# Two side-by-side products for 13 blocks of a split-float decoder kernel

## The chip, the cores and the metric

The kernel is one program on one core of a Trainium2 chip. The metric is the device time of that program in microseconds (us). The engines are TensorE (PE, with its weight loads shown as PEld), VectorE (DVE), ScalarE (ACT), GpSimd (POOL) and SyncE (SP), which issues most DMAs.

## The reference, cut to what matters

Two decoder blocks run over 256 tokens with a model width of 2048, in float32. Everything heavy is a product of activations with a weight matrix:

```python
proj = xn @ w_in                                   # hgrn_qf, hgrn_v, gate_q_k, idx_q, attn_v ...
h = h + jnp.concatenate([y_h, y_a], axis=-1) @ w_out       # mix_out
h = h + memory_cross_attention(...)                # cross_q, cross_k, cross_v, cross_out
h = h + sqrelu_mlp(rms_norm(h, norm_mlp), w_up, w_down)    # up0..3, down0..3
# second block: pooling mixer (pool_*, out0), shared keys and values of a sparse attention
kv = (hn @ w_kv)                                   # cmp_kv, sel_k, sel_v, win_k, win_v
q = hn @ w_b[:, :1536]                             # nsa_q, 3 blocks
```

RMS norms stand before the products. The kernel multiplies by the norm's factor of each token behind the product, when it reads the result.

## The kernel before

**Blocks and units.** The weights pass through the core once, in 95 blocks, one after the other in the order of `plan_stream`. A dense block is 2048 rows by 512 columns of a weight matrix (4 MB). It comes in 4 DMAs of 1 MB into 4 slots of `ring` (SP, `stream`, L474), each 4 row tiles of 128 rows by 512 columns, so a run of 2 KB per row. A block is worked on in 8 units of 2 row tiles. For each unit ACT rounds the weights into `w_high` (`high_unit`, L1244), POOL subtracts to get the rest, `w_low` (`low_parts`, L628, line L654, in 2 pieces of 512 elements per partition or 4 of 256), and PE multiplies. `w_high` and `w_low` have 4 places (`UNITS`), so ACT starts unit n when PE is done with unit n - 4 (`units_used`), and DMA of a ring slot starts when POOL is done with it (`low_ready`).

**The products.** A float32 product is made of three products of rounded parts: w_high x_high + w_high x_low + w_low x_high (`accumulate`, L687 is its matmul). In a features unit (L691) the weights are the stationary operand and the 256 tokens stream: 2 row tiles x 4 feature tiles x 3 products = 24 matmuls of 256 columns, 192 per block. In a tokens unit the tokens are stationary and 512 features stream: 12 matmuls of 512 columns, 96 per block.

**Groups.** The sums of a dense block stand in 2 banks of PSUM, 256 tokens x 4 feature tiles. That is a group, and groups take turns on two pairs of banks (`pair_of`). Before PE begins group g it waits until group g - 2 has been read out (`group_free`, L671, semaphore `evacuated`). DVE reads a group out with two operations of 512 elements (`read_out` L1691, called by `keep` L1699, lines L1736 and L1731; or `residual_group` L1750, which adds to `hT`).

**Order around the change.** Each engine runs its own written list. In `hgrn_qf` (4 blocks, the first work of the kernel) DVE can read out the first group only when the norm's factor is known: `norm_sum` (L792, lines L795 and L797) stands in PE's list before unit 4 of block 1, ACT makes the root (L1288, L1289), and DVE waits for it (`scale_known`). In the second half DVE's list reads `keep("cmp_kv")`, `rope_angles`, `build_blocks(0)` (L2352), `low_blocks(0)` (L2362, which waits for ACT's L1596), `keep("sel_k")`, `build_blocks(1)`, `low_blocks(1)`, `keep("sel_v")`, two `rotate` (L2322 to L2326), `keep("win_k")`. In `nsa_q` (3 blocks) DVE rotates queries (`rotate`) after each block; the first attention steps on PE (L818) wait for the last two.

Of the kernel before, what the change touches and what calls it, by code (L numbers as in the profile page):

```python
# [12 lines left out]
P = 128  # L13
# [35 lines left out]
class Gemm:  # L49
# [6 lines left out]
    def __init__(self, b0, blocks, g0, groups, rows, width):  # L56
        self.b0, self.blocks, self.g0, self.groups, self.rows, self.width = b0, blocks, g0, groups, rows, width
        self.units = 8 * blocks // groups

# [4 lines left out]
    def unit(self, u):  # L64

        half = (self.rows + 1) // 2
        return (0, half) if u % 2 == 0 else (half, self.rows - half)


def plan_stream():  # L70
# [12 lines left out]
    for name, blocks, groups, *shape in order:  # L83
        plan[name] = Gemm(b, blocks, g, groups, *(shape or (4, 512)))
        b += blocks
        g += groups
# [3 lines left out]
def build_program(nc, a):  # L90
    PLAN = plan_stream()
    ctx = ExitStack()
    with ctx:
# [14 lines left out]
        x_high = sb("x_high", [P, KT, T], F32R)  # L108
        x_low = sb("x_low", [P, KT, T], F32R)
# [347 lines left out]
        def _(sp):  # L457
# [16 lines left out]
            def stream(name, source):  # L474
# [3 lines left out]
                def block_of(n, b, more):  # L478
                    for j in range(4):

                        need = 8 * b + 2 * j - 2 * RING + 2
                        if need > 0:
                            sp.wait_ge(low_ready, need + more)
                        dst = ring[:, j, 0:g.rows * g.width].rearrange("p (k n) -> p k n", k=g.rows)
# [8 lines left out]
                peel = g.blocks if g.blocks < 3 or name == "out0" else int(g.b0 == 0)  # L493
# [6 lines left out]
            def columns(w, col0):  # L500
# [3 lines left out]
                return lambda n, j: w3[:, 4 * j:4 * j + 4, bass.ds(n * 512 + col0, 512)]  # L504
# [49 lines left out]
            stream("out0", lambda n, j: out0_part(n, GATED_FIRST[j]))  # L554
# [115 lines left out]
        def _(pe):  # L670
# [33 lines left out]

            def tokens_unit(g, b, u, pair, x, first, of, more=0):
# [27 lines left out]
            def product(name, unit, x, made=None, ready=x_ready, sums=None, begun=0, sums_at=7):  # L733
# [3 lines left out]
                def block_of(n, more, more_groups, wait):  # L737
                    group_free(g.g0 + n, more_groups)
                    for u in range(8):
# [4 lines left out]
                        unit(g, g.b0 + n, u, pair_of(g.g0 + n), x, 4 * (u // 2), KT, more)  # L744

                peel = g.blocks if g.blocks < 4 else (begun if made is None else 2)
# [115 lines left out]
            def one_unit(name, k):  # L862

                g, n, u = PLAN[name], k // 8, k % 8
                if u == 0:
# [35 lines left out]
            for n in range(4):  # L901
                group_free(g.g0 + n)
                for u in range(8):
                    if n == 0:
                        pe.wait_ge(rows_kept, u + 1)
                    if n == 1 and u == 4:
                        norm_sum(pair_tile(16, 16), columns=True)
                    features_unit(g, g.b0 + n, u, pair_of(g.g0 + n), operand, 4 * (u // 2), KT)
# [298 lines left out]
            def turn_h(i):  # L1207

                pe.wait_ge(evacuated, PLAN["out0"].g0 + 4)
# [21 lines left out]
        def _(act):  # L1231
# [72 lines left out]
            def norm_turn(name, slot, cols, squares=scratch, freed=0, begun=0):  # L1304
# [3 lines left out]
                for u in range(8):  # L1308
# [3 lines left out]
                    elif u == 0:  # L1312
                        act.wait_ge(evacuated, g.g0 + 3)
# [5 lines left out]
                act.wait_ge(evacuated, g.g0 + 4)  # L1319
# [143 lines left out]
            for c in range(2):  # L1463
                act.wait_ge(evacuated, c + 1)
                act.activation(hg_gates[:, c, :], pair_tile(4 * c, 4), ACT.Sigmoid).then_inc(hg_act, 1)
                high(1)
            for c in range(2):
                act.wait_ge(evacuated, c + 3)
# [213 lines left out]
        def _(dve):  # L1682
# [8 lines left out]
            def read_out(g, q, i, put):  # L1691

                n = g.g0 + q
# [5 lines left out]
            def keep(name, dst):  # L1699
# [812 lines left out]
```

## Time and profile before

| | us |
|---|---|
| median of 3 runs | 2368.94 (2368.47 to 2369.37) |
| the profiled execution | 2373.35 |
| its span (first to last instruction) | 2371.6 |
| PE busy | 2300.8 |
| POOL busy | 2076.7 |
| ACT busy | 1072.3 |
| DVE busy | 934.6 |

1.75 us of the profiled execution lie outside its span. Engines run at the same time, so busy times don't add up. Matmuls are pipelined: each shows the time from its start to the end of its last column, and the next starts well before that; what a matmul costs in a row of them is the distance from start to start. The granted clock is PE's: 1.00 is 2.4 GHz and 0.50 is 1.2 GHz.

### The profile page before, as it was taken

The page shows a single profiled execution, that of the slowest core. Times are in us where ns is not written, and L with a number is a line of the kernel's source. Part 1 is how long each engine was busy: PE and PEld are TensorE (multiplying, and loading weights), DVE is VectorE, ACT ScalarE, POOL GpSimd, SP SyncE. Part 2 cuts the span into 40 slices and gives each one's busy share as a digit, 9 for nine tenths or more (in the row PEclk, how much of TensorE's full clock was granted, in tenths as well). Part 3 has the DMA queues.
Part 4 walks back from the last instruction along what each step waited for, and adds up shares of the span by engine and source line. Part 5 has one row for each costly group of instructions (what it writes and reads, how often), then busy time and mean ns, then how long its engine had stood idle before and what let it go on. Part 6 is the DMA issues. An engine that isn't in the chain of part 4 may idle for free. (4 is left out here: it accounts for less than half of the span.)

```text
span 2371.6 us, 38269 instructions
## 1 busy us (share of the span) xinstructions
PE 2300.8 (97%) x14870; PEld 2082.1 (88%) x14870; DVE 934.6 (39%) x1389; ACT 1072.3 (45%) x1412; POOL 2076.7 (88%) x1933
## 2 busy tenths in 40 slices
PE   8999999999999999999999999999999998999998
PEld 8989998788997888888888888999899987999886
DVE  5165665765053620120120121522514555465522
ACT  5443334474365533333333333544445445455553
POOL 8999998797996899999999999898999898875587
PEclk9999999999999999999999999999999999999999
DMA  6654444353543456565655555554455556543343
GB/s 233 186 168 147 157 144 151 143 194 126 196 160 125 152 186 202 189 194 187 188 193 188 187 192 178 165 188 151 144 197 189 176 167 201 166 154 107 107 160 124
DMA packets 207143, 401.09 MB, mean 169 GB/s; under 512 B 10515, under 2 KB 21013, under 8 KB 206357
## 3 DMA queue, kind: packets, MB, share of 16 engines
q1 hardware_dynamic: 206628, 398.45, 52.2%
q8 instruction: 104, 1.70, 0.3%
q10 hardware_dynamic: 368, 0.59, 0.1%
q14 instruction: 43, 0.34, 0.1%
HBM read 396.92 MB, written 2.10 MB: 168 GB/s over the span
## 5 line engine op out<-in xcount | busy, mean ns | idle before, releaser
L654 POOL TENSOR_TENSOR w_low<-ring,w_high 128x512 fp32r<-128x512 f32 (+3 forms) x1868 | 2067.5, 1132 | 278.2 <-ACT w_high L1253 217.8
L1253 ACT ACTIVATE w_high<-ring 128x1024 fp32r<-128x1024 f32 (+2 forms) x760 | 788.9, 1040 | 1206.7 <-PE bank L687 1192.8
L687 PE MATMUL bank<-x_high,w_high 128*128 128x256 f32 x2948 | 850.8, 289 | 23.3 <-POOL w_low L654 11.6
L687 PE MATMUL bank<-x_low,w_high 128*128 128x256 f32 x2948 | 836.5, 284 | 0.0
L687 PE MATMUL bank<-x_high,w_low 128*128 128x256 f32 x2948 | 836.5, 284 | 0.0
L687 PEld LDWEIGHTS bank<-x_high,w_high 128*128 128x128 f32 x2948 | 565.7, 192 | 32.7 <-issue 21.4
L687 PEld LDWEIGHTS bank<-x_low,w_high 128*128 128x128 f32 x2948 | 566.0, 192 | 0.9 <-issue 0.5
L687 PEld LDWEIGHTS bank<-x_high,w_low 128*128 128x128 f32 x2948 | 565.7, 192 | 0.1
L687 PE MATMUL bank<-w_high,x_high 128*128 128x512 f32 x928 | 373.2, 402 | 7.4 <-POOL w_low L654 4.3
L687 PE MATMUL bank<-w_low,x_high 128*128 128x512 f32 x928 | 363.3, 391 | 0.0
L687 PE MATMUL bank<-w_high,x_low 128*128 128x512 f32 x928 | 363.0, 391 | 0.0
L687 PE MATMUL bank<-w_high,hidden 128*128 128x512 f32 x960 | 296.2, 390 | 0.0
L687 PEld LDWEIGHTS bank<-w_high,x_high 128*128 128x128 f32 x928 | 175.1, 189 | 54.3 <-issue 7.4
L687 PEld LDWEIGHTS bank<-w_high,hidden 128*128 128x128 f32 x960 | 179.7, 188 | 37.1
L687 PEld LDWEIGHTS bank<-w_low,x_high 128*128 128x128 f32 x928 | 174.9, 188 | 37.5
L687 PEld LDWEIGHTS bank<-w_high,x_low 128*128 128x128 f32 x928 | 175.1, 189 | 37.0 <-issue 2.9
L687 PE MATMUL bank<-w_low,hidden 128*128 128x512 f32 x480 | 186.9, 389 | 0.0
L1736 DVE TENSOR_TENSOR proj<-bank,scale_all 128x512 f32<-128x512 f32 (+1 forms) x62 | 39.8, 683 | 179.7 <-PE bank L687 178.0
L1792 DVE SCALAR_TENSOR_TENSOR x_low<-hT,gains,x_high 128x256 fp32r<-128x256 f32 x80 | 93.2, 1217 | 36.7 <-ACT x_high L1300 36.5
L687 PEld LDWEIGHTS bank<-w_low,hidden 128*128 128x128 f32 x480 | 90.1, 188 | 18.8
L2209 DVE TENSOR_SCALAR heads_scratch<-bank,scale_all 128x512 f32<-128x512 f32 x32 | 22.6, 747 | 202.4 <-issue 194.3
L1744 DVE TENSOR_TENSOR proj<-bank,proj 128x512 f32 (+1 forms) x22 | 14.2, 686 | 181.1 <-PE bank L687 181.1
(299 smaller groups left out, 1740.2 us busy)
## 6 DMA issues: line engine op xcount, KB each, us to landing
ring<-in_w_in SPq DMA_DIRECT2D x64, 1024.0 KB, 5.4
ring<-in_w_up SPq DMA_DIRECT2D x64, 1024.0 KB, 5.2
ring<-in_w_down SPq DMA_DIRECT2D x64, 1024.0 KB, 5.1
ring<-in_w_out SPq DMA_DIRECT2D x48, 1024.0 KB, 5.1
ring<-in_a_w_in SPq DMA_DIRECT2D x32, 1024.0 KB, 5.3
ring<-in_b_w_in SPq DMA_DIRECT2D x32, 1024.0 KB, 5.4
ring<-in_w_kv SPq DMA_DIRECT2D x24, 1024.0 KB, 5.2
ring<-in_w_mem_kv SPq DMA_DIRECT2D x16, 1024.0 KB, 5.1
```

The source lines that it names most:

```text
L654: last = pool.tensor_tensor(w_low[:, u % UNITS, part], ring[:, u // 2, first:first + n], w_high[:, u % UNITS, part], ALU.subtract)
L687: mm = pe.matmul(out, lhs, rhs, start=start and n == 0, stop=stop and n == 2, skip_group_check=True)
L1253: act.activation(w_high[:, u % UNITS, 0:n], ring[:, u // 2, r0 * g.width:r0 * g.width + n], ACT.Copy)\
L1736: return lambda n, c, b: dve.tensor_tensor(proj[:, bass.ds(n * 4 + (t0 + 2 * c), 2), :], two(b), scale_two, ALU.mult)
L1744: return lambda n, c, b: dve.tensor_tensor(v[:, c, bass.ds(n * 512, 512)], b[:, :], v[:, c, bass.ds(n * 512, 512)], ALU.add)
L1792: last = dve.scalar_tensor_tensor(out=x_low[:, t, :], in0=hT[:, t, :], scalar=gains[:, slot, cols.start + t:cols.start + t + 1], in1=x_hig ...
L2209: last = dve.tensor_scalar(up_rows[:, h, :], bank[2 * ((g.g0 + q) % 2) + h][:, :], scale_col(h), 0.0, ALU.mult, ALU.max)
```

## The change

Thirteen of the features blocks become wide: blocks 1, 2, 3 of `hgrn_qf`; 1, 2 of `mix_out`; 1, 2 of `out0`; 1 of `cmp_kv`; `sel_k`; `win_k`; and 0, 1, 2 of `nsa_q`. `x_high` and `x_low` become two halves of one tensor `x_parts`. A wide unit has 4 row tiles of 256 features in place of 2 row tiles of 512. For each row tile and feature tile w_high streams x high and low in one matmul of 512 columns, into a whole bank (high in columns 0 to 255, low in 256 to 511), and w_low streams x_high into columns 0 to 255: 16 matmuls per unit.

```diff
+WIDE = {"hgrn_qf": (1, 2, 3), "mix_out": (1, 2), "out0": (1, 2), "cmp_kv": (1,), "sel_k": (0,), "win_k": (0,),
+        "nsa_q": (0, 1, 2)}
...
+            def wide_unit(g, n, u):
+
+                half, v = divmod(u, 4)
+                if v == 0:
+                    group_free(g.group(n) + half)
+                pe.wait_ge(low_ready, 8 * (g.b0 + n) + u + 1)
...
+                for k in range(4):
+                    kt = 4 * v + k
+                    for f in range(2):
+                        cols = slice(f * P, f * P + P)
+                        pe.matmul(pair[f][:, :].rearrange("p (a t) -> p a t", a=2), wh[:, k, cols], x_parts[:, :, kt, :],
+                                  start=(kt == 0), stop=(kt == KT - 1), skip_group_check=True)
+                        mm = pe.matmul(pair[f][:, 0:T], wl[:, k, cols], x_high[:, kt, :], start=False,
+                                       stop=(kt == KT - 1), skip_group_check=True)
+                mm.then_inc(units_used, 1)
```

A wide block has two groups of 256 features, one for units 0 to 3 and one for units 4 to 7, so `group_free` is asked in the middle of a block too, and the block's sums fill 4 banks in turn rather than 2. DVE reads a wide group out with 4 operations of 256 elements that scale, a wait for them, and 2 that add high and low (`read_wide`), or, into `hT`, with 2 adds, a wait and 2 adds:

```diff
+            def read_wide(g, n, t0, factor=None):
+
+                for half in range(2):
+                    pair = pair_rows(g.group(n) + half)
+                    t = t0 + 4 * n + 2 * half
+                    dve.wait_ge(units_used, 8 * (g.b0 + n) + 4 * half + 4)
+                    for b, f in ((pair[0], 0), (pair[1], 1)):
+                        for dst, src in ((proj[:, t + f, :], b[:, T:2 * T]), (b[:, 0:T], b[:, 0:T])):
+                            if factor is None:
+                                last = dve.tensor_tensor(dst, src, scale_rows_, ALU.mult)
...
+                    then(last)
+                    for f in range(2):
+                        last = dve.tensor_tensor(proj[:, t + f, :], pair[f][:, 0:T], proj[:, t + f, :], ALU.add)
+                    last.then_inc(evacuated, 1)
```

The ring DMAs of wide blocks bring 8 row tiles x 256 columns, so runs of 1 KB, 1 MB each as before. Blocks of `mix_out`, `out0`, and the others named are written out instead of looped on PE, SP and DVE. The waits that counted groups (`evacuated`) are renumbered.

Two places of the new order. On PE, the middle of block 1 of `hgrn_qf` (units 3 and 4), before:

```order
L687 MATMUL bank3<-x_high,w_high 128x256
L687 MATMUL bank3<-x_low,w_high 128x256
L687 MATMUL bank3<-x_high,w_low 128x256
L795 MATMUL bank4<-proj,ones 128x256 [waits norm_folded]
L797 MATMUL bank4<-ones,proj 128x2 x2
L687 MATMUL bank2<-x_high,w_high 128x256 [waits low_ready]
L687 MATMUL bank2<-x_low,w_high 128x256
L687 MATMUL bank2<-x_high,w_low 128x256
```

The same place after the change:

```order
L741 MATMUL bank3<-x_parts,w_high 128x512
L743 MATMUL bank3<-x_parts,w_low 128x256
L841 MATMUL bank4<-proj,ones 128x256 [waits norm_folded]
L843 MATMUL bank4<-ones,proj 128x2 x2
L741 MATMUL bank0<-x_parts,w_high 128x512 [waits low_ready,evacuated]
L743 MATMUL bank0<-x_parts,w_low 128x256
```

Unit 4 went on in banks 2 and 3 and waited for its weights alone; now it begins a group in banks 0 and 1 and waits for `evacuated` as well, which is the read-out of block 0.

On DVE, from the end of `build_blocks(0)` to the start of `build_blocks(1)`, before:

```order
L2352 TENSOR_TENSOR heads_scratch<-proj,pe_cols 128x16x15 x7
L2362 TENSOR_TENSOR block_parts_50<-heads_scratch,block_parts_50 128x1920 [waits blocks_high]
L1731 SCALAR_TENSOR_TENSOR proj<-bank0,scale_all 128x512 [waits units_used]
L1731 SCALAR_TENSOR_TENSOR proj<-bank1,scale_all 128x512
L2352 TENSOR_TENSOR heads_scratch<-proj,pe_cols 128x16x15 [waits x_ready,evacuated]
```

and after:

```order
L2438 TENSOR_TENSOR heads_scratch<-proj,pe_cols 128x16x15 x7
L2448 TENSOR_TENSOR block_parts_50<-heads_scratch,block_parts_50 128x1920 [waits blocks_high]
L1763 SCALAR_TENSOR_TENSOR proj<-bank0,scale_all 128x256 [waits units_used]
L1763 SCALAR_TENSOR_TENSOR bank0<-bank0,scale_all 128x256
L1763 SCALAR_TENSOR_TENSOR proj<-bank1,scale_all 128x256
L1763 SCALAR_TENSOR_TENSOR bank1<-bank1,scale_all 128x256
L1767 TENSOR_TENSOR proj<-bank0,proj 128x256 [waits dve_order]
L1767 TENSOR_TENSOR proj<-bank1,proj 128x256
L1763 SCALAR_TENSOR_TENSOR proj<-bank2,scale_all 128x256 [waits units_used]
```

The read-out of `sel_k` keeps its place in DVE's list and grows from 2 operations to 12, in two groups. `sel_k` was one group, so the block behind it, `sel_v`, waited for the last group of `cmp_kv`; now `sel_k` is two groups, and `sel_v` waits for the first of them.

## Rows read from the trace of the kernel before

**Rows 1.** Page, part 1: engine, busy us (share of span), instructions
```profile
PE 2300.8 (97%) x14870; PEld 2082.1 (88%) x14870; DVE 934.6 (39%) x1389; ACT 1072.3 (45%) x1412; POOL 2076.7 (88%) x1933
```

**Rows 2.** Windows: stretch, length, busy us (count) by engine, PE clock, DMA share, GB/s
```profile
65.43:88.47 23.04, 23.04 (x195) 23.04 (x193) 1.29 (x2) 8.49 (x8) 21.43 (x18) 1.00 0.62 188
952.43:974.20 21.77, 21.77 (x98) 18.02 (x97) 1.29 (x2) 8.49 (x8) 20.28 (x17) 1.00 0.62 193
1846.73:1870.78 24.05, 23.96 (x198) 23.39 (x196) 1.76 (x3) 10.16 (x11) 22.90 (x18) 1.00 0.55 176
1893.91:1919.80 25.89, 22.92 (x98) 17.52 (x97) 18.47 (x15) 15.77 (x15) 22.12 (x15) 1.00 0.51 163
1919.80:1944.15 24.35, 23.81 (x192) 23.30 (x193) 10.12 (x11) 7.43 (x7) 23.72 (x17) 1.00 0.51 161
```

**Rows 3.** Timeline of POOL, mix_out to cross_q: start, us, operation [idle before, releaser]
```profile
631.25 2.55 POOL L654 TENSOR_TENSOR w_low<-ring,w_high 128x512 fp32r<-128x512 f32 x2 [0.16 <-POOL w_low L654]
...
661.56 6.09 POOL L654 TENSOR_TENSOR w_low<-ring,w_high 128x512 fp32r<-128x512 f32 x6 [0.16 <-POOL w_low L654]
```

**Rows 4.** Timeline of POOL, then of PE, in cross_q
```profile
662.81 30.33 POOL L654 TENSOR_TENSOR w_low<-ring,w_high 128x512 fp32r<-128x512 f32 x34
...
689.57 0.36 PE L687 MATMUL bank<-x_high,w_high 128*128 128x256 f32 x1 [0.22 <-POOL w_low L654]
```

**Rows 5.** Timelines of PE, ACT and DVE around unit 4 of hgrn_qf's block 1
```profile
52.58 0.28 PE L687 MATMUL bank<-x_high,w_low 128*128 128x256 f32 x1
52.94 0.70 PE L795 MATMUL bank<-proj,ones 128*128 128x256 f32 x2
53.47 0.50 PE L797 MATMUL bank<-ones,proj 128*128 128x2 f32 x4
53.84 0.36 PE L687 MATMUL bank<-x_high,w_high 128*128 128x256 f32 x1
...
55.27 0.48 ACT L1288 ACTIVATE scale_all<-bank,eps_col 128x260 f32<-128x260 f32 x1
55.76 1.28 ACT L1289 ACT_TABLE_LOAD   x1
57.06 0.42 ACT L1289 ACTIVATE scale_all<-scale_all 128x260 f32<-128x260 f32 x1
...
57.83 1.29 DVE L1736 TENSOR_TENSOR proj<-bank,scale_all 128x512 f32 x2 [1.54 <-ACT scale_all L1289]
```

**Rows 6.** Timelines of DVE, ACT and PE from the end of cmp_kv into sel_v
```profile
1870.31 1.29 DVE L1736 TENSOR_TENSOR proj<-bank,scale_all 128x512 f32<-128x512 f32 x2 [22.02 <-PE bank L687]
...
1894.23 1.81 ACT L1596 ACTIVATE block_parts<-heads_scratch 128x1920 fp32r<-128x1920 f32 x1 [4.82 <-DVE heads_scratch L2352]
...
1896.08 2.16 DVE L2362 TENSOR_TENSOR block_parts<-heads_scratch,block_parts 128x1920 fp32r<-128x1920 f32 x1 [1.88 <-ACT block_parts L1596]
1898.15 1.28 DVE L1731 SCALAR_TENSOR_TENSOR proj<-bank,scale_all 128x512 f32<-128x512 f32 x2
...
1901.05 0.50 PE L687 MATMUL bank<-w_high,x_high 128*128 128x512 f32 x1 [1.50 <-POOL w_low L654]
```

**Rows 7.** Groups by line and form, DVE reading PSUM: count, busy us, mean ns, idle before
```profile
L1863 DVE SCALAR_TENSOR_TENSOR x_low<-bank,gains,x_high 128x256 fp32r<-128x256 f32 x64 | 27.7, 477 | 41.2 <-ACT x_high L1399 40.9 <-DVE x_low L1863 0.2
L1935 DVE COPY proj<-bank 128x256 f32<-128x256 f32 x32 | 13.4, 419 | 43.4 <-PE bank L858 43.3
```

**Rows 8.** Windows and timeline of PE around an idle stretch before nsa_q, columns as in 2 and 3
```profile
2003.20:2006.40 3.20, 0.00 (x0) 0.00 (x0) 0.42 (x1) 1.51 (x2) 2.48 (x2) 1.00 1.05 395
2007.40:2010.80 3.40, 3.40 (x19) 3.40 (x18) 0.00 (x0) 1.31 (x2) 3.24 (x4) 0.50 0.93 305
2010.80:2013.70 2.90, 2.90 (x26) 2.90 (x25) 0.00 (x0) 1.06 (x1) 2.74 (x3) 0.99 0.93 321
...
2006.47 0.35 PE L687 MATMUL bank<-x_high,w_high 128*128 128x256 f32 x1 [3.27 <-POOL w_low L654]
```

**Rows 9.** Timelines of DVE and PE from the last group of nsa_q to attention
```profile
2084.20 1.29 DVE L1736 TENSOR_TENSOR proj<-bank,scale_all 128x512 f32<-128x512 f32 x2 [11.56 <-PE bank L687]
...
2092.58 1.11 DVE L2326 TENSOR_TENSOR proj<-rstd 32x512 f32<-32x512 f32 x1
...
2093.75 0.92 PE L818 MATMUL bank<-proj 128*128 128x128 f32 x4 [0.51 <-DVE proj L2326]
```

**Rows 10.** DMA issues: count, KB each, median us to landing; and an ACT wait for one
```profile
ring<-in_w_kv SPq DMA_DIRECT2D x24, 1024.0 KB, 5.2
ring<-in_cmp_w SPq DMA_DIRECT2D x8, 1024.0 KB, 5.6
...
2002.70 2.00 ACT L1253 ACTIVATE w_high<-ring 128x1024 fp32r<-128x1024 f32 x2 [2.02 <-DMA ring<-in_b_w_in]
```

**Rows 11.** Timeline of DVE behind hgrn_qf: the last group, and the wait for PE
```profile
111.84 1.29 DVE L1736 TENSOR_TENSOR proj<-bank,scale_all 128x512 f32 x2 [21.75 <-PE bank L687]
...
147.68 0.77 DVE L2017 COPY_PREDICATED heads_scratch<-ident,bank 128x512 f32<-128x512 int32 x1 [9.21 <-PE bank L919]
```

More of the change, by code:

```diff
@@ L58, in __init__, with group, ended @@
         self.units = 8 * blocks // groups
+        self.wide = ()
+    def group(self, n):
+        return self.g0 + n + sum(1 for w in self.wide if w < n)
+    def ended(self, n):
+        return self.group(n + 1)
     def made(self, n=0):
@@ L553, in _ @@
             out0_part = columns(w_out2[0:D, :], 0)
-            stream("out0", lambda n, j: out0_part(n, GATED_FIRST[j]))
+            stream("out0", lambda n, j, wide=False: out0_part(n, j if wide else GATED_FIRST[j], wide))
             w_kv = a["w_kv_2"]
@@ L737, in block_of @@
                 def block_of(n, more, more_groups, wait):
-                    group_free(g.g0 + n, more_groups)
+                    if n in g.wide:
+                        for u in range(8):
+                            wide_unit(g, n, u)
+                        return
+                    group_free(g.group(n), more_groups)
                     for u in range(8):
@@ L743, in block_of @@
                             pe.wait_ge(ready, made + u // 2 + 1)
-                        unit(g, g.b0 + n, u, pair_of(g.g0 + n), x, 4 * (u // 2), KT, more)
-                peel = g.blocks if g.blocks < 4 else (begun if made is None else 2)
+                        unit(g, g.b0 + n, u, pair_of(g.group(n)), x, 4 * (u // 2), KT, more)
+                peel = g.blocks if g.blocks < 4 or g.wide else (begun if made is None else 2)
                 for n in range(begun, peel):
@@ L1752, in residual_group @@
                 g = PLAN[name]
+                if j in g.wide:
+                    for half in range(2):
+                        pair = pair_rows(g.group(j) + half)
+                        dve.wait_ge(units_used, 8 * (g.b0 + j) + 4 * half + 4)
+                        for part in range(2):
+                            for f in range(2):
+                                h = hT[:, 4 * j + 2 * half + f, :]
+                                last = dve.tensor_tensor(h, pair[f][:, part * T:part * T + T], h, ALU.add)
+                            if part == 0:
+                                then(last)
+                        last.then_inc(evacuated, 1)
+                    return
                 dve.wait_ge(units_used, g.made(j))
```

72 lines of the change are left out of this document (48 added, 24 removed).

## Prediction

> **What bounds the kernel now.** I read the page's busy times first: PE is busy 97% of the span and POOL 88% [rows 1]. So PE's list sets the time, with POOL close behind. Then the windows of single blocks, for the price of a matmul. In a features block 192 matmuls of 256 columns take 23.04 us, 0.120 us each; in a tokens block 96 of 512 columns take 21.77 us, 0.2268 us each [rows 2]. Twice the columns cost 0.1068 us more, so a matmul costs 0.1068 us per 256 columns and 0.0132 us for being one. The chain of waits has little in it but PE; what counts is where PE would wait, so I went along the 13 blocks and asked of each new wait in PE's list when it ends, by the timelines of the engine waited for.
>
> **Term 1, the matmuls.** A row tile and feature tile cost 3 x 0.120 = 0.360 us before, and 0.2268 + 0.120 = 0.3468 after, 0.0132 less. A dense block has 64 such pairs: 0.85 us, 22.19 in place of 23.04. Thirteen blocks give 11.0 us if nothing else moves. No row shows a stream made of two pieces of 256 columns; its bounds are 0.2268 (like one piece) and 0.240 (like two matmuls). I take the first, since one instruction and one load are issued.
> The Trainium skill has a rule against this term ("TensorE: Matmul & The Clock Gate", "Back-to-back issue gap"): a matmul in a warm stream costs its columns and about 2.5 ns. By it the pair would save 2.5 ns, 64 x 13 of them 2.1 us. These rows have 13.2 ns, for 256 and for 512 columns alike, so the trace disagrees with it here.
>
> **Term 2, a wait inside hgrn_qf.** Unit 4 of block 1 now opens a group in the banks of block 0, so PE waits for DVE to read block 0 out. DVE can't before the norm's factor is there, and `norm_sum` stands right before that wait in PE's own list. In the rows: PE issues it at 52.94, ACT's root ends at 57.48, DVE reads out from 57.83 to 59.12, and PE went on at 53.84 [rows 5]. The old kernel needed this read-out only at 65.4, at block 2. In the new one PE reaches unit 4 0.4 us sooner (four units at 2.77), which ACT can use for its table load, so the read-out ends near 58.7, and PE resumes at 58.75: 4.9 us of idle PE. Behind the wait stand all later matmuls; ACT and POOL are at most four units ahead, so they stop too. Idle PE has a second price. After 3.27 us of idle PE the granted clock was 0.50 for 3.4 us, 19 matmuls ran in that stretch against 26 in the 2.9 us behind it [rows 8]; at 0.50 a stretch of 3.4 us does the work of about 1.9, so 1.5 us. Sum for the stage: 4.9 + 1.5 - 3 x 0.85 = **+3.9 us**. The read-out of the last group is 1.2 us longer (term 5), but the next PE work that needs DVE starts at 147.7 after DVE had waited 9.2 us for PE [rows 11], so that stays covered.
>
> **Term 3, mix_out and out0.** Four blocks, 3.4 us at most. POOL is the cover to check. Its unit in these loops takes 2.55 and 0.16 of wait, 2.71 [rows 3]; PE's new unit takes 2.77, so POOL still keeps ahead, by 0.06 instead of 0.17 a unit. In `out0` POOL has since saturated its four places before `cmp_kv` needs them, so its 1.7 us stay. Behind `mix_out` stands `cross_q`, where POOL works without a gap from 662.81 for 30.33 us and PE waits 0.22 us for it [rows 4]. POOL had slack (the 0.16 waits are its own, the pieces from 652.9 on waited for PE) of about 0.8 us to start that stretch sooner. So PE gets 1.7 sooner to that wait and loses 0.9 there. I take **-0.8** for `mix_out` and **-1.7** for `out0`.
>
> **Term 4, sel_v waits for sel_k.** `cmp_kv` block 1 saves 0.85. But `sel_v` must now wait for the first half of `sel_k` to be read out, and in DVE's list this stands behind `rope_angles`, `build_blocks(0)` and `low_blocks(0)`. Before, that read-out began at 1898.15 [rows 6], while `sel_v` began at 1893.91 [rows 2] and needed only `cmp_kv`. New times, with S for the shift of PE at the end of `cmp_kv`: its own last group takes 1.2 us longer (term 5), so the chain read-out, angles, blocks, ACT L1596, L2362 ends at 1899.4 + S; six operations of 0.40 us and a wait, 2.5 us; PE starts `sel_v` at 1902.0 + S. It would be ready at 1870.78 + 22.19 = 1893.0 + S: 9 us idle, and 1.5 for the clock. From there: `sel_v` 21.77, `win_k` 22.19, together 1947.6 + S, if POOL keeps up. POOL has some 36 us of subtractions from `sel_v` unit 4 on and can't start them before 1907.2, so it is just in time; I add 0.5. Before, `win_k` ended at 1944.15 [rows 2]. That is +4.0 + S, S = -0.85: **+3.15 us**. It is less than the 9 us of the stall because the old kernel lost 4.1 us in `sel_v` (25.89 against 21.77) and 1.3 in `win_k` (24.35 against 23.04) to POOL and ACT [rows 2, 6], and these waits go: POOL works ahead during the stall. The savings of `sel_k` and `win_k` are in the sum. The work behind is paced by PE's units and by ACT, and keeps the shift.
>
> **Term 5, DVE.** A group of 512 elements x 2 takes 1.29 us [rows 6]. A 256-element operation reading PSUM takes 0.42 (copy) to 0.48 us (three operands) alone [rows 7], in a row some 0.40 to 0.43: six of them 2.4 and a semaphore round 0.1, so 2.5 per wide group, 1.2 more behind the last unit. Per wide block DVE does 5.0 us instead of 1.3. DVE has 39% of work [rows 1] and these operations lie beside matmuls, except behind a last group. That counts in `nsa_q`: the last group, two rotations, and the attention step that waits 0.51 us for them [rows 9]. So of the 3 x 0.85 saved there 1.2 go back. The cover elsewhere, if gone, costs PE a wait at `group_free` of at most that 2.5 us per place.
>
> **Term 6, DMA.** Runs of 1 KB in place of 2: `cmp_w`, which has such runs, lands in 5.6 us, `w_kv` in 5.2 [rows 10]. Where slots are refilled a block ahead that is nothing. At the start of `nsa_q` ACT waited 2.02 us for a landing and PE for ACT [rows 8, 10], so I charge 0.5 us. With term 5, `nsa_q`: -2.55 + 1.2 + 0.5 = **-0.8**. Renumbered waits, unrolled loops and the common tensor of x cost nothing that a row shows: sequencers wait there anyway; at most a few tenths.
>
> **Sum.** 3.9 - 0.8 - 1.7 + 3.15 - 0.8 = +3.75. On the profiled execution: span 2371.6 + 3.75, and 1.75 outside it, 2377.1. The median of the runs is 4.41 below that execution (2368.94 against 2373.35), so **2372.7 us**.
>
> **The rivals.**
> A, as forecast: both stalls come and eat the gain. Its own range is 2369 to 2377: no clock loss at either stall takes 3.0 off, POOL not held up in `cross_q` 0.9; and on the other side the clock staying low twice as long adds 3.0 and a late POOL behind `sel_v` 1.
> B, the stalls are largely absorbed. The place is `sel_v`: everything from there to `nsa_q` is paced by POOL and by ACT's place in its list, so PE ahead of them is worth nothing, and PE late costs nothing until POOL's four places are full. If `win_k` then ends where it ended (term 4 gives -0.85 or 0 instead of +3.15) and the wait in `hgrn_qf` costs no clock, the time is 2372.7 - 4.0 - 1.5 - 1.5 = 2366; with a shorter root chain 2363. For it: POOL leads by only 0.1 us in that stretch. Against: a 9 us hole is longer than the 5.4 us of waits that it can replace.
> C, slower: the two-piece stream costs like two matmuls, 0.240. Then term 1 is gone everywhere it counted, some 8 to 9 us, and the stalls stay: 2381. Each 0.001 us more on a stream costs 64 x 10 blocks of it, 0.64 us, so it decides from 0.2284 on, where the time passes 2373.7. For it: nothing shows such a stream. Against: it is one instruction.
> By the Trainium skill's rule of term 1 ("TensorE: Matmul & The Clock Gate", "Back-to-back issue gap"), the saving is 2.1 us in place of 11.0 and the time nearly the same as in C, 2381; the rows against it are [rows 2], and I give it 2 of C's 10 in a hundred.
> D, slower: the read-outs of wide groups cost more than 2.5 us, since half of them write back into PSUM, which no row shows; at 4 us each the three chains behind last groups (`cmp_kv`, `sel_k`, `nsa_q`) lose 1.5 to 3 us each: 2378.
> E, the change does what it says and the wait in `hgrn_qf` is shorter, for example as ACT's root is earlier: no place in the rows for it, since ACT did it as soon as its table was loaded.
>
> **How the numbers follow.** A 0.55, B 0.17 (with E), C 0.10, D 0.18. A measurement of this kernel can tell about 0.2% from no change, 4.7 us: below 2364.2 is faster, above 2373.7 slower. A lies two thirds below 2373.7 and one third above; B is a third faster and else the same; C and D are slower. With some weight for unseen gains: faster 0.12, same 0.47, slower 0.41. The range leaves out the far end of B, and C: 2364 to 2380.5.
>
> **What would show it right or wrong.** The timeline of PE must show some 5 us idle before unit 4 of `hgrn_qf` block 1 near 54 us, released by DVE, and some 9 us before `sel_v`, each followed by a few us at clock 0.50. Wide blocks without waits must take 22.2 us; 23.0 would be C. DVE's groups of wide blocks must take near 2.5 us; 4 would be D. If `win_k` ends no later relative to `cmp_kv` than before, B holds. Where a wide block in `nsa_q`, `mix_out` or `out0` begins a group late, a cover that I counted on is gone.

## The result and the profile after

The changed kernel takes 2375.22 us (median of 12 runs, 2372.48 to 2378.5), the one before 2371.29 us in the same comparison (12 runs, 2368.47 to 2374.59). The ratio is 1.0016, 95% interval 1.0009 to 1.0024: slower by 0.16%, 3.9 us, where the prediction had +3.75 us. The forecast time was 2372.7 us, inside its range of 2364 to 2380.5 and 2.5 below the median; 2.35 of that is the kernel before itself, 2368.94 in three runs ahead of the prediction and 2371.29 here. The profiled execution after has a span of 2373.4 us, 1.8 us more than the one before. The two differences need not agree: executions of one kernel differ by several us here, and below I say which part of that the traces show.

The busy times first, as in [rows 1]:

```profile
PE 2293.9 (97%) x14038; PEld 2038.2 (86%) x14038; DVE 962.7 (41%) x1503; ACT 1073.0 (45%) x1412; POOL 2076.7 (87%) x1933
```

832 matmuls have gone and PE is busy 6.9 us less, in a kernel that takes longer. So PE waits more. The waits of PE over the whole program (line that waited, who released it: us in total, times, longest):

```profile
PE bank L711 <- POOL w_low L678: 11.0, 16, 1.4
PE bank L711 <- DVE proj L1767: 7.9, 1, 7.9
...
PE bank L741 <- DVE proj L1810: 4.7, 1, 4.7
...
PE bank L741 <- POOL w_low L678: 2.9, 1, 2.9
```

Two single waits for DVE are new, 4.7 and 7.9 us. The waits for POOL, 17.2 us in 21 places before, are 13.9 now. Then the windows by block (columns as in [rows 2]): block 1 and 2 of `hgrn_qf`, `mix_out` 1, `cmp_kv` 1, `sel_k`, `sel_v`, `win_k`:

```profile
40.20:71.58 31.38, 26.43 (x136) 22.64 (x135) 15.63 (x15) 15.34 (x16) 23.50 (x17) 0.89 0.46 136
71.58:93.77 22.19, 22.19 (x130) 19.40 (x129) 4.36 (x12) 8.50 (x8) 20.70 (x18) 1.00 0.62 190
604.45:627.06 22.61, 22.61 (x130) 19.62 (x129) 2.79 (x6) 8.50 (x8) 21.34 (x18) 1.00 0.62 200
...
1848.62:1871.94 23.32, 23.19 (x134) 19.65 (x132) 3.94 (x10) 10.19 (x11) 22.17 (x18) 1.00 0.56 180
1871.94:1902.32 30.38, 22.46 (x131) 19.55 (x128) 28.13 (x31) 13.35 (x17) 26.03 (x19) 0.91 0.54 173
1902.32:1926.32 24.00, 24.00 (x96) 19.64 (x97) 8.94 (x15) 9.13 (x8) 19.22 (x16) 0.91 0.43 133
1926.32:1948.92 22.60, 22.60 (x129) 19.61 (x128) 13.94 (x19) 8.49 (x8) 22.05 (x16) 1.00 0.55 180
```

Read the length, PE's busy time and the clock together. `hgrn_qf` 2 is the clear case, 22.19 us with PE busy all the time. `mix_out` 1 is as clear and takes 22.61. In block 1 of `hgrn_qf` and in `sel_k` PE is busy 5 and 8 us less than the block is long, and the clock falls below 1.00. By stages, from the first matmul of one block to the first of another:

| stage | before | after | difference | predicted |
|---|---|---|---|---|
| hgrn_qf 1 to 3 | 70.33 | 75.76 | +5.43 | +3.9 |
| mix_out 1, 2 with 3 and cross_q | 96.19 | 96.09 | -0.1 | -0.8 |
| out0 1, 2 with 3 and cmp_kv 0 | 93.19 | 93.05 | -0.1 | -1.7 |
| cmp_kv 1 to win_k | 97.42 | 100.30 | +2.88 | +3.15 |
| nsa_q with nsa_zq 0 | 110.62 | 108.23 | -2.39 | -0.8 |

These are +5.7 us together. The rest of the way to +1.8 lies in blocks that the change does not touch: `attn_v` 0 took 40.57 us before and 38.42 after, as a stretch at clock 0.50 near 386 us is missing after; the first block began 1.25 us sooner behind its first DMA; `cmp_hid_k` and the gates are 0.6 us shorter. The stretch before, with PE's clock at 0.76 on the mean of it:

```profile
383.00:390.00 7.00, 5.08 (x13) 3.69 (x14) 2.08 (x1) 4.79 (x6) 6.84 (x11) 0.76 0.58 179
```

That one need not be chance. In all 13 traces of the changed kernel and its versions below, `attn_v` 0 takes 38.3 to 38.9 us and the clock does not fall there; PE's wait for ACT, 2.07 us before, is 1.3 to 1.7 in twelve of them and 2.0 in that of run 4. The start of block 1 of `hgrn_qf`, 41.2 before and 40.2 after, lies anywhere from 39.8 to 42.2 us in these traces.

**The wait in hgrn_qf**, to be held against [rows 5]. Timelines of PE, ACT and DVE:

```profile
51.97 0.70 PE L841 MATMUL bank<-proj,ones 128*128 128x256 f32 x2 [0.29 <-DVE proj L1895]
52.50 0.50 PE L843 MATMUL bank<-ones,proj 128*128 128x2 f32 x4
57.67 0.79 PE L741 MATMUL bank<-x_parts,w_high 128*128 128x512 f32 x1 [4.67 <-DVE proj L1810]
...
55.87 0.42 ACT L1342 ACTIVATE scale_all<-scale_all 128x260 f32<-128x260 f32 x1
...
56.33 1.29 DVE L1810 TENSOR_TENSOR proj<-bank,scale_all 128x512 f32<-128x512 f32 x2 [1.00 <-ACT scale_all L1342]
```

And the window behind the wait:

```profile
57.70:63.60 5.90, 5.90 (x19) 5.03 (x20) 2.00 (x6) 0.35 (x1) 0.64 (x1) 0.50 0.61 178
```

The norm's sum, the root, the read-out, and then unit 4, 5.7 us after the norm matmul began; before, unit 4 followed it by 0.9 us. That window has 5.9 us at clock 0.50, so 3 us are lost there on top of the 4.67 of idle time.

**The wait before sel_v**, against [rows 6]. DVE and PE:

```profile
1871.47 0.42 DVE L1761 TENSOR_TENSOR proj<-bank,scale_all 128x256 f32<-128x256 f32 x1 [8.88 <-PE bank L743]
...
1885.21 10.91 DVE L2438 TENSOR_TENSOR heads_scratch<-proj,pe_cols 128x240 f32<-128x240 f32 x8
1897.99 2.16 DVE L2448 TENSOR_TENSOR block_parts<-heads_scratch,block_parts 128x1920 fp32r<-128x1920 f32 x1 [1.87 <-ACT block_parts L1649]
1900.06 0.42 DVE L1763 SCALAR_TENSOR_TENSOR proj<-bank,scale_all 128x256 f32<-128x256 f32 x1
...
1901.52 0.75 DVE L1767 TENSOR_TENSOR proj<-bank,proj 128x256 f32<-128x256 f32 x2
...
1902.32 1.22 PE L711 MATMUL bank<-w_high,x_parts 128*128 128x512 f32 x2 [7.92 <-DVE proj L1767]
```

DVE has no idle time between `cmp_kv` and this read-out but for 1.87 us, and PE starts `sel_v` when its first half is out. A wide group takes 1900.06 to 1902.27, 2.2 us.

### The profile page after: what moved, and what is told of

The parts are those of the page before. It is cut to its first block and busy times, and to the rows that moved or that the text cites. A ratio compares the mean times of both kernels' runs of the same rounds, so it can differ in the third digit from the quotient of the medians.

```text
span 2373.4 us, 36567 instructions
## 1 busy us (share of the span) xinstructions
PE 2293.9 (97%) x14038; PEld 2038.2 (86%) x14038; DVE 962.7 (41%) x1503; ACT 1073.0 (45%) x1412; POOL 2076.7 (87%) x1933
## 5 line engine op out<-in xcount | busy, mean ns | idle before, releaser
L711 PE MATMUL bank<-x_parts,w_high 128*128 128x256 f32 x4232 | 782.2, 287 | 16.7 <-POOL w_low L678 7.0
L711 PEld LDWEIGHTS bank<-x_parts,w_high 128*128 128x128 f32 x4232 | 660.0, 192 | 25.6 <-issue 14.1
L711 PE MATMUL bank<-x_parts,w_low 128*128 128x256 f32 (+1 forms) x2116 | 600.0, 284 | 0.0
L711 PE MATMUL bank<-w_high,x_parts 128*128 128x512 f32 x1856 | 585.4, 397 | 13.8 <-DVE proj L1767 7.9
L711 PEld LDWEIGHTS bank<-w_high,x_parts 128*128 128x128 f32 x1856 | 346.0, 189 | 96.9 <-issue 10.0
L711 PEld LDWEIGHTS bank<-x_parts,w_low 128*128 128x128 f32 (+1 forms) x2116 | 405.0, 191 | 0.1
L711 PE MATMUL bank<-w_low,x_parts 128*128 128x512 f32 x928 | 363.2, 391 | 0.0
L741 PE MATMUL bank<-x_parts,w_high 128*128 128x512 f32 x832 | 296.8, 401 | 7.7 <-DVE proj L1810 4.7
L743 PE MATMUL bank<-x_parts,w_low 128*128 128x256 f32 x832 | 233.9, 281 | 0.0
L711 PEld LDWEIGHTS bank<-w_low,x_parts 128*128 128x128 f32 x928 | 175.0, 189 | 37.6
L741 PEld LDWEIGHTS bank<-x_parts,w_high 128*128 128x128 f32 x832 | 157.5, 189 | 46.0 <-DVE proj L1810 4.8
```

The source lines that it names most:

```text
L711: mm = pe.matmul(out, lhs, rhs, start=start and n == 0, stop=stop and n == 2, skip_group_check=True)
L741: pe.matmul(pair[f][:, :].rearrange("p (a t) -> p a t", a=2), wh[:, k, cols], x_parts[:, :, kt, :], start=(kt == 0), stop=(kt == KT - 1), ...
L743: mm = pe.matmul(pair[f][:, 0:T], wl[:, k, cols], x_high[:, kt, :], start=False, stop=(kt == KT - 1), skip_group_check=True)
```

## The experiments

In runs 1 to 8 the time is that of one execution, the profiled one, and single executions of one kernel lie up to 6 us apart. So stages are compared, not whole times: a whole time carries stretches at half clock that come and go.

**1. Block 1 of hgrn_qf narrow.**

```diff
-WIDE = {"hgrn_qf": (1, 2, 3),
+WIDE = {"hgrn_qf": (2, 3),
...
-                if n == 0:
-                    group_free(g.g0)
+                if n not in g.wide:
+                    group_free(g.group(n))
...
```

> Block 1 of hgrn_qf is narrow again; 12 blocks stay wide. My theory (PE idles for the read-out of block 0 and then runs at half clock): that block takes 24.3 us as before the change, not 31.4, so the stage is 7.1 us shorter, no 4.7 us hole near 53 us, clock 1.00 there; blocks 2 and 3 keep 22.2 to 22.6 us. The half-clock stretch in attn_v near 386 us that the changed kernel lacks may return, 2 us, so 5 to 7 us less in all than the changed kernel. Rival (the hole is only work moved, and ACT and POOL catch up behind it): hgrn_v starts at most 1 us sooner.

Time 2369.73 us. The window of blocks 1 to 3:

```profile
40.49:109.97 69.48, 69.41 (x457) 63.14 (x455) 21.36 (x29) 36.33 (x36) 64.62 (x50) 1.00 0.60 183
```

69.48 us against 75.76, without idle time and at clock 1.00. Making this one block wide costs 6.3 us net. Two wide blocks without it are 0.85 us better than before the change. The wait for the read-out is shown as the cause: without it `hgrn_v` starts 6 us sooner, where the rival allowed 1. I had expected 7.1; blocks 2 and 3 took 22.61 and 22.62 us in this kernel instead of 22.19 (section 8 is on that). The stretch at half clock in `attn_v` that might have returned did not.

**2. sel_k narrow.** In `WIDE`:

```diff
-        "sel_k": (0,),
```

> sel_k is narrow again, one group; 12 blocks stay wide. From the start of cmp_kv block 1 to the start of win_v the kernel before took 97.4 us and the changed one 100.3. My theory (sel_v waits for a read-out that stands late in VectorE's list): no hole before sel_v, the POOL and ACT waits of 4 to 5 us in sel_v and win_k are back, and the stretch takes 97.5 us, 2.8 less. Rival (VectorE's longer read-outs as such cost the time, by delaying its chain): sel_k's own read-out is a third of them, so the stretch stays above 99 us.

Time 2367.89 us. From `cmp_kv` 1 to the start of `win_v`:

```profile
1842.74:1939.94 97.20, 93.60 (x550) 81.41 (x549) 59.43 (x62) 40.93 (x43) 90.48 (x65) 0.98 0.53 170
```

97.20 us, 3.1 less than after the change and 0.2 less than before it. The rival, over 99 us, falls. With `cmp_kv` 1 and `win_k` still wide, 0.9 to 1.7 us should have been gained; `sel_v` took 26.57 and `win_k` 24.18, so POOL and ACT keep it, as rival B had said of that stretch.

**3. What part of the price is the clock.** Matmuls whose results nobody reads keep PE busy during the two waits, 8 in the first and 14 in the second.

```diff
+            def fill(to, count):
+                for i in range(count):
+                    pe.matmul(bank[to][:, 0:T], ones[:, :], hT[:, i, :], start=True, stop=True, skip_group_check=True)
...
+                if g is PLAN["hgrn_qf"] and n == 1 and u == 4:
+                    fill(6, 8)
...
+            fill(7, 14)
             product("sel_v", tokens_unit, operand)
```

> The changed kernel with PE kept at work in its two holes: 8 matmuls of ones with a tile of hT into an unused bank before the wait in hgrn_qf block 1, and 14 before sel_v. Nothing reads them. My theory (a hole costs its own length and then a stretch at half clock): the holes end at the same times, the clock stays at 1.00, hgrn_qf block 1 takes 31.4 - 3 = 28.4 us and sel_v 24.0 - 2 = 22 us, 5 us less in all. Rival (the clock falls for another reason, or the half-clock stretch is hidden by waits behind it): block 1 within 0.5 us of 31.4.

Time 2371.4 us. Block 1 of `hgrn_qf`, and `sel_v`:

```profile
40.70:69.37 28.67, 27.28 (x153) 23.29 (x151) 15.61 (x15) 15.34 (x16) 23.49 (x17) 1.00 0.50 150
...
1898.13:1921.67 23.54, 23.54 (x97) 19.27 (x97) 9.94 (x15) 9.14 (x8) 19.44 (x16) 0.93 0.44 137
```

In `hgrn_qf` the clock stayed at 1.00 and the block took 28.67 us instead of 31.38: 2.7 us of the price were the clock, 4.7 the wait itself. Before `sel_v` it worked in part only: the fillers ended before the wait did, PE was idle for 1.9 us, 3.4 us at 0.50 followed, and `sel_v` took 23.54 instead of the 22.0 that I expected. That half is inconclusive.

**4. Wide groups, but three matmuls.** w_high streams x high and low in two matmuls of 256, all else as changed.

```diff
-                        pe.matmul(pair[f][:, :]..., wh[:, k, cols], x_parts[:, :, kt, :],
-                                  start=(kt == 0), stop=(kt == KT - 1), ...)
+                        pe.matmul(pair[f][:, 0:T], wh[:, k, cols], x_high[:, kt, :],
+                                  start=(kt == 0), stop=False, ...)
+                        pe.matmul(pair[f][:, T:2 * T], wh[:, k, cols], x_low[:, kt, :],
+                                  start=False, stop=(kt == KT - 1), ...)
```

> The changed kernel with its layout, groups, DMAs, waits and read-outs, but w_high streams x_high and x_low in two matmuls of 256 columns: 24 matmuls per unit as before the change. My theory (the pair of streams saves 7 to 13 ns, the price of one instruction, the rest of the change only costs): clear wide blocks take 23.04 us instead of 22.19 or 22.61; the kernel is 4 to 8 us slower than the changed one, about 2381, the holes stay. Rival (the 256-column and two-half layout saves the time): the blocks stay near 22.2 to 22.6.

Time 2377.51 us. Clear wide blocks took 23.04 us, as narrow ones, so the groups of 256 features and the 1 KB runs of the DMAs cost PE nothing there, and the whole gain is the saved matmul. The time is 2.3 us above the changed kernel's median, less than the 4 to 8 that I expected, since one of the two holes, which were to stay, nearly closed. Three other stages taught more. `cross_q` and `cmp_kv` 0 went back to 27.10 and 24.07 us, from 27.82 and 24.79: what they lost after the change came with an earlier PE (run 7 adds to this for `cmp_kv` 0). `nsa_zq` 0 stayed at 33.52 (33.09 before, 33.56 after), so the 0.4 to 0.5 us there are the longer read-out and its rotations. And the wait before `sel_v` shrank from 7.9 to 2.1 us, which no theory had; `sel_k` took 25.79 us instead of 30.38. The window of `sel_k` in this kernel, then timelines of DVE and POOL in it:

```profile
1874.56:1900.35 25.79, 23.55 (x196) 23.14 (x193) 21.54 (x31) 12.39 (x15) 25.16 (x16) 1.00 0.52 163
```
```profile
1887.09 3.95 DVE L2440 TENSOR_TENSOR heads_scratch<-proj,pe_cols 128x240 f32<-128x240 f32 x8
...
1886.85 5.31 POOL L678 TENSOR_TENSOR w_low<-ring,w_high 128x512 fp32r<-128x512 f32 x1
```

The same eight operations of `build_blocks(0)` that took 10.91 us after (and 10.93 before) take 3.95 here, while one subtraction of POOL takes 5.31 instead of some 1.3. After the change DVE and POOL took turns, one operation each, at 1.36 us per operation of DVE (10.91 for eight), and POOL's took 1.4 to 1.5; here DVE went through in one go and POOL stood. What decides between the two was not tried. By the Trainium skill ("Advanced Engine Details and Errata", "GPSIMD Details") the Pool engine shares a read and a write interface with VectorE and conflicts, among others, with its instructions of two SBUF inputs; the eight operations of DVE here read two tensors in SBUF, `proj` and `pe_cols`, and the rows agree, while read-outs, which take one input from PSUM, stay at 0.42 us beside POOL.

**5. The read-outs of sel_k earlier in DVE's list.** `read_wide` gets the halves that it reads.

```diff
             rope_angles()
+            read_wide(PLAN["sel_k"], 0, 8, -ATT_SCALE, (0,))
             build_blocks(0)
             low_blocks(0)
-            keep("sel_k", scaled_keys(8), 8, -ATT_SCALE)
+            read_wide(PLAN["sel_k"], 0, 8, -ATT_SCALE, (1,))
```

> Everything as changed, with only the read-outs of sel_k moved earlier in the list of DVE (first half ahead of build_blocks(0), second behind low_blocks(0)). Theory: the idle time ahead of sel_v falls from 7.9 us to 6 to 7 us, the stretch from cmp_kv 1 to win_v from 100.3 to 99 to 100 us. Rival (order does not matter): 100.3 again.

Time 2376.42 us, with clock stretches elsewhere that the stage does not contain. The windows of `sel_k` and `sel_v`, and PE's longest wait in them:

```profile
1874.25:1896.55 22.30, 22.30 (x131) 19.66 (x129) 21.92 (x27) 7.56 (x11) 21.67 (x17) 1.00 0.58 190
1896.55:1924.35 27.80, 23.89 (x99) 18.94 (x97) 20.36 (x21) 15.50 (x15) 22.99 (x16) 0.94 0.45 151
```
```profile
PE bank L711 <- POOL w_low L678: 3.1, 1, 3.1
```

`sel_k` runs through in 22.30 us, and the stage takes 97.39 us instead of 100.30; I had expected 99 to 100. PE no longer waits for DVE there, where I expected 6 to 7 us of it, but for POOL, 3.1 us and then 0.8. I had thought that the second half of `sel_k` would hold `sel_v` as the first had, but `sel_v` needs only the first. The place of the first read-out in DVE's list is the cause of that hole. But 97.39 us is what the stage took before the change (97.42) and with `sel_k` narrow (97.20): closing the hole brings the stage back to where it was, and POOL keeps what the wide blocks save.

**6. Blocks 1 and 2 of out0 with three matmuls.** The edit of 4, only where `g is PLAN["out0"]`.

> In blocks 1 and 2 of out0 alone w_high streams x high and low in two matmuls again (24 per unit, in wide groups); all else as changed. Theory (cmp_kv 0 waits for the norm chain of DVE, ACT and PE, whose end does not depend on how fast out0 runs): blocks 1 and 2 of out0 take 23.04 us each instead of 22.61, cmp_kv 0 takes 24.07 instead of 24.79, so the stretch from out0 1 to cmp_kv 1 is 93.2 us, as before the change (93.2) and 0.1 us above the changed kernel (93.06). Rival (the 0.72 us in cmp_kv 0 come from the longer read-outs of the wide blocks): cmp_kv 0 stays at 24.8 and the stretch grows to 93.9.

Time 2377.05 us. `out0` 1, and `cmp_kv` 0:

```profile
1754.76:1777.80 23.04, 23.04 (x195) 23.04 (x194) 2.80 (x6) 8.47 (x8) 21.77 (x18) 1.00 0.63 199
1823.88:1847.95 24.07, 24.07 (x200) 23.92 (x199) 20.20 (x16) 13.63 (x18) 20.72 (x13) 1.00 0.52 173
```

As the theory said, 93.19 us from `out0` 1 to `cmp_kv` 1, 0.14 more than after the change. What `out0` gained, `cmp_kv` 0 gave back. In the changed kernel the place is PE's wait before the norm of `cmp_kv`:

```profile
1844.77 0.70 PE L841 MATMUL bank<-scratch,ones 128*128 128x256 f32 x2 [0.61 <-DVE scratch L1895]
```

**7. The order of the four matmuls of a row tile.**

```diff
                     for f in range(2):
                         pe.matmul(pair[f]..., wh..., x_parts...)
-                        mm = pe.matmul(pair[f][:, 0:T], wl..., x_high...)
+                    for f in range(2):
+                        ...
+                        mm = pe.matmul(pair[f][:, 0:T], wl..., x_high...)
```

> Within a row tile the two matmuls of 512 columns go first and the two of 256 behind them, instead of 512, 256, 512, 256; all else as changed. Theory (each matmul costs its columns plus about 13 ns whatever stands next to it): four matmuls take 692 to 708 ns as now, clear wide blocks 22.2 to 22.6 us. Rival (a short matmul behind a long one hides part of its weight load, and two short ones in a row do not): four matmuls take over 710 ns, blocks over 22.7.

Time 2371.24 us. `mix_out` 1, and `cross_q`:

```profile
603.03:625.33 22.30, 22.30 (x131) 19.46 (x129) 2.80 (x6) 8.51 (x8) 21.03 (x18) 1.00 0.62 202
670.66:699.39 28.73, 25.48 (x208) 24.84 (x207) 11.84 (x13) 15.01 (x20) 26.21 (x32) 1.00 0.42 147
```

Every clear wide block takes 22.29 to 22.30 us in this order (`hgrn_qf` 2 and 3, `mix_out`, `out0`, `nsa_q` 2), four matmuls 697 ns. The rival, that it would be dearer, falls. The gain of `mix_out` is lost in `cross_q`, which takes 28.73 us, with 1.6 us of waits for POOL against 0.8 after and 0.2 before. The gain of `out0` is kept here: `cmp_kv` 0 took 24.01. That contradicts the theory of run 6, that the end of the norm chain does not move. The operations that make x low on DVE tell the two apart, groups of the stretch 1740 to 1850 us, before, after, and in this kernel:

```profile
L1792 DVE SCALAR_TENSOR_TENSOR x_low<-hT,gains,x_high 128x256 fp32r<-128x256 f32 x16 | 19.1, 1238 | 12.7 <-ACT x_high L1300 12.7
```
```profile
L1878 DVE SCALAR_TENSOR_TENSOR x_parts<-hT,gains,x_parts 128x256 fp32r<-128x256 f32 x16 | 23.1, 1514 | 9.1 <-ACT x_parts L1353 9.0
```
```profile
L1880 DVE SCALAR_TENSOR_TENSOR x_parts<-hT,gains,x_parts 128x256 fp32r<-128x256 f32 x16 | 18.8, 1216 | 12.7 <-ACT x_parts L1355 12.7
```

After the change 16 operations took 4.0 us longer and DVE ran ten of them without idle time. This is DVE and POOL again, in a wasteful phase after the change and in a good one here. The other traces say the same: `cmp_kv` 0 takes 24.7 to 24.8 us in all seven with the order 512, 256 in `out0`, and 24.0 to 24.1 in the three with the order of this run. That the phase makes the 0.7 us is argued from these rows, not shown by a run that sets it.

**8. Two prices of a pair.** In the changed kernel a pair (one matmul of 512, one of 256) takes 346 to 347 ns in `hgrn_qf` 2 and 3, most of `cmp_kv` 1 and `sel_k`, and 353 ns on the mean in `mix_out`, `out0`, `win_k` and `nsa_q` 2: 22.19 and 22.61 us a block. To see what chooses, each wide group got one extra matmul ahead of it, of 16 to 224 columns.

```diff
+                if v == 0:
+                    cut = 32 * (1 + g.group(n) % 7) if half == 0 else 16 * (1 + g.group(n) % 5)
+                    pe.matmul(pair[0][:, 0:cut], wh[:, 0, 0:P], x_high[:, 0, 0:cut], start=True, stop=True, ...)
```

> Ahead of the first matmul of each wide group stands one extra matmul that writes 16 to 224 columns of the group's own bank, which the group then overwrites; its width differs from group to group (first halves 32 to 224 columns, second halves 16 to 80). It shifts the time at which the stream of pairs begins and adds under 0.1 us per group. Two prices of a pair (one matmul of 512 columns and one of 256) were seen: 346 ns and 353 ns. Theory A (the price depends on how the stream was entered, and holds until it is broken): groups behind some widths run at 346 ns, behind others at 353 ns, in the same blocks that showed one price alone. Theory B (the price depends on what POOL, ACT and the DMAs do in that block): mix_out, out0 and win_k stay at 353 ns in all groups, blocks 2 and 3 of hgrn_qf at 346 ns.

Time 2378.73 us. Mean distance of pairs, ns, behind the first unit of a group, with the width of the extra matmul:

| block | first half: width, price | second half: width, price |
|---|---|---|
| hgrn_qf 2 | 128, 346 | 64, 353 |
| hgrn_qf 3 | 192, 353 | 16, 347 |
| mix_out 1 | 160, 353 | 16, 353 |
| mix_out 2 | 224, 353 | 48, 346 |
| out0 1 | 192, 353 | 48, 353 |
| out0 2 | 32, 346 | 80, 353 |
| nsa_q 2 | 192, 353 | 64, 346 |

Blocks that had shown one price throughout now show the other in one half. So the price belongs to how the stream of pairs was entered and holds until it is broken (theory A); what POOL, ACT and DMA do in the block does not fix it (B falls). Run 5 says the same without an extra matmul: its program is the changed kernel's up to `cmp_kv`, yet blocks 2 and 3 of `hgrn_qf` took 22.62 and 22.61 us in its execution, not 22.19. The width alone does not fix it either: 64 and 48 columns stand beside both. What inside PE it is stays open. In the grouped order of run 7 there is one price only.

**9. Versions put together.** With the two wide blocks that cost more than they bring made narrow again (WIDE without block 1 of `hgrn_qf` and without `sel_k`):

> Block 1 of hgrn_qf and the block sel_k go back to narrow, the other 11 blocks stay wide. Theory (two stalls cost more than the whole saving): without block 1 of hgrn_qf the kernel gets 6.3 us back (stretch of blocks 1 to 3 at 24.25 + 2 x 22.6 = 69.5 against 75.8), without sel_k 3.1 us (stretch from cmp_kv 1 to win_v at 97.2 against 100.3). From +3.9 of the changed kernel over the one before that gives -5.5 us, a ratio of 0.9977 and a time near 2366. Rival (the gains of single blocks are given back later, at the next wait of PE): the sum of the two is smaller than of each alone, ratio 0.9985 or more.

2368.75 us against 2371.56, ratio 0.9984 (0.9975 to 0.9993). `hgrn_qf` 1 to 3 took 69.5 us, `cmp_kv` 1 to `win_k` 97.3, as each change alone. The expected 0.9977 and the rival's 0.9985 both lie inside the interval; the stages, not the ratio, say that the two gains add. With `sel_k` wide and its read-outs early instead:

> Block 1 of hgrn_qf narrow; sel_k wide, but its two halves are read out earlier in the list of DVE: the first ahead of build_blocks(0), the second behind low_blocks(0), so that DVE frees the banks of sel_v sooner. Theory (the hole ahead of sel_v is the place of the read-out in the list of DVE): the stretch from cmp_kv 1 to win_v shrinks from 100.3 to 99 to 100 us, not to 97.2, since the second half still stands behind low_blocks(0). Time 4 us above nothing: -2.3 - 0.8 = -3 us against the kernel before, ratio 0.9987. Rival (the hole is set by the work of DVE and not by its order): stretch unchanged at 100.3, ratio 0.9990.

2367.71 us, ratio 0.9982 (0.9973 to 0.9991). That is not to be told from the last one, since the stage took 97.6 us, less than expected. Then this with the order of run 7:

> The three repairs together: block 1 of hgrn_qf narrow, sel_k read out early (first half ahead of build_blocks(0), second behind low_blocks(0)), and the matmuls of a row tile ordered 512, 512, 256, 256. Theory (they act at different places, so their gains add): the version with the first two was at 0.9982; the grouped order gave clear wide blocks of 22.29 instead of 22.61 us, 10 such blocks, less what cross_q gives back, so 2 to 3 us more: ratio 0.9971. Rival (the last gain is given back at the next wait of PE): 0.9982 again.

2365.31 us against 2372.05, ratio **0.9975** (0.9966 to 0.9984), 6.7 us below the kernel before and, by the two ratios, about 10 below the changed one. The expected 0.9971 and the rival's 0.9982 both lie inside the interval. And the same with `mix_out` narrow:

> As the version with all three repairs, with blocks 1 and 2 of mix_out narrow too. Theory (in cross_q POOL is the limit, so what PE gains in mix_out is lost there: 2 x 0.75 gained, 1.66 lost): the stretch from mix_out 1 to cross_k takes within 0.2 us of the same, the ratio is the same as of the version with mix_out wide. Rival (the loss in cross_q has another cause): the stretch is 1.5 us longer.

2366.85 us, ratio 0.998 (0.9971 to 0.9989); the two medians are 1.5 us apart, and the intervals overlap by more than half, so they don't tell the two apart. The windows from `mix_out` 1 to `cross_out`, with it wide and narrow:

```profile
599.66:762.75 163.09, 153.96 (x1029) 139.44 (x1028) 58.61 (x87) 85.33 (x122) 138.68 (x147) 1.00 0.48 158
```
```profile
596.52:759.52 163.00, 155.16 (x1157) 146.47 (x1155) 54.52 (x75) 85.29 (x122) 138.87 (x147) 1.00 0.48 158
```

128 matmuls more and the stretch is as long. POOL is busy 138.7 and 138.9 us in both. So the two wide blocks of `mix_out` bring nothing in this stretch.

## Why the prediction was right, and where it was not

Forecast A came: both stalls arrive and eat the gain, +3.9 us against +3.75. Some of its terms missed, and part of the agreement is luck.

**Term 1, the matmuls.** 22.19 us, as worked out, in `hgrn_qf` 2 and 3, and 22.61 in the other clear blocks: the saving is 0.85 or 0.42 us a block. Rival C, a two-piece stream at the price of two, did not come. What failed was the assumption that a pair has one price. By the formula of the Trainium skill ("TensorE: Matmul & The Clock Gate", "Back-to-back issue gap"), a matmul's columns at 2.4 GHz and 2.5 ns, the saving would be an estimated 0.16 us a block; both measured ones are above it. The prediction took this for a rule against its term. The same section calls the formula the gap of an isolated matmul and says that in a stream of weight loads and matmuls both set the spacing, so it was not a rival for this stream.

**Term 2, hgrn_qf.** The idle time was 4.7 us, predicted 4.9, by the predicted chain. The clock was mis-sized: I took 3.4 us at 0.50 and a loss of 1.5, from one place where PE had been idle 3.3 us (its own counts, 19 matmuls against 26 in 2.9 us, give 2.1 us of work and a loss of 1.3); here it was 5.9 us of work at 0.50, a loss of 3, and run 3 gives 2.7. The stage cost +5.4 instead of +3.9. In run 2 the same wait was followed by only 3.4 us at 0.50 and the block took 30.00 us, so the loss varies from execution to execution.

**Term 3, mix_out and out0.** Both failed: -0.1 and -0.1 for -0.8 and -1.7. In `cross_q` the step was right in kind (POOL is the limit), but the gain was halved by the pair's price and nothing was left, as the last two versions of section 9 show. For `out0` the step that POOL "has since saturated its four places before `cmp_kv` needs them, so its 1.7 us stay" looked at the wrong engine: DVE and its norm chain in `cmp_kv` 0 were late next, by 0.6 us of waiting for it in PE's list and, as run 7 argues, by how DVE met POOL there. The prediction had named a lost cover only in general; this was one.

**Term 4, sel_v.** +2.9 for +3.15, with the hole 7.9 us for 9 and 2.2 us for the clock in place of 1.5 (`sel_v` took 24.00 against 21.77). `win_k` took 22.60 us without a wait to speak of, so POOL did catch up during the hole, and the 0.5 us added for it was not needed; that the dearer pair took 0.4 us of it in `win_k` is luck. (The sum has a slip too: 1902.0 + 1.5 + 21.77 + 22.19 is 1947.5, not 1947.6.) Runs 2 and 5 show the cause.

**Term 5 and nsa_q.** A wide group takes 2.2 us, predicted 2.5: its operations start 0.33 us apart, not 0.40, and the wait among them is 0.04 us, not 0.1, which no row had shown. Rival D, 4 us for writing back into PSUM, did not come: these operations take 0.42 us, like the ones that write SBUF. `nsa_q` with what follows shows -2.4, but 1.5 of it is a stretch at 0.50 that the profiled execution after does not have at 2010; in runs 2, 5 and 6, which have it, `nsa_q` 0 takes 28.8 to 28.9 us against 29.30, and the stage is at -0.9, predicted -0.8. Here the agreement is luck: the three blocks gained 1.4 us, not 2.55, and what follows lost 0.5, not 1.7.

**The sum.** With -0.9 for `nsa_q`, the stages give +7.2, 3.4 more than predicted, and the blocks nearby another -0.6. The medians moved by 3.9. The 2.2 us of `attn_v` 0 would bring that to +4.4, if they belong to the change; one trace of the kernel before can't show it. What lies between I can't assign: how long PE stays at 0.50 behind each wait differs between executions, and the medians run over more of them than the traces. So the place and kind of the two stalls is shown, the size +3.9 is measured, and that the sum met it is partly luck.

## What to carry to other kernels

Before work is split into more groups, ask for each buffer that now comes free earlier in the list who frees it and where that stands in *its* list: here a saving of 0.4 to 0.85 us per block was outweighed by two read-outs that stood behind other work, and one of them needed only a new place in DVE's list to go, though the stage was then no faster than before the change. Price an idle PE by the wait and by the slow stretch behind it, up to twice what one quiet example shows. And when PE gains time ahead of a stage where POOL or DVE is the limit, count the gain as zero until the trace of that stage shows slack.

## What the runs showed of the hardware that was not expected

- A pair of a 512-column and a 256-column matmul, alternating, takes 346 or 353 ns; which one is set when the stream begins and stays through units and blocks. In the order 512, 512, 256, 256 four take 697 ns in every clear wide block, 348 per pair.
- DVE and POOL meet in two ways when DVE's operations have two SBUF inputs: DVE's eight operations in 10.91 us with POOL at 1.4 to 1.5 us each, or in 3.95 us with one operation of POOL stretched to 5.31. DVE's and POOL's lists are the same in both kernels; only PE's matmuls, and so the times at which they meet, differ.
- Idle PE of 2 to 5 us was followed by 3.4 or 6.8 us at 0.50 or by nothing, at the same place of programs that are the same there: after 2.9 us of idle time at 2010 us the clock stayed at 1.00 in the changed kernel's execution, and after 2.8 us there it fell to 0.50 for 3.4 us in that of run 5. Eight matmuls into an unused bank held it at 1.00 through a wait of 4.7 us.
